# Softplus of the time step on 128 partitions of 68 elements, by way of DRAM, spread over tiles four to ten

## The reference, cut to what matters

```python
xn = rmsnorm(h, lw['norm_mix'])
proj = xn @ lw['w_in']
z, xbc, dt, gate, xl = jnp.split(proj, [s1, s2, s3, s4], axis=-1)
...
dt = jax.nn.softplus(dt + lw['dt_bias'])        # 544 tokens x 16 heads
a = -jnp.exp(lw['a_log'])
y, ssd_h = ssd_chunked(xs, dt, a, bm, cm, ssd_h0)
...
# in ssd_chunked
da = (dt * a).reshape(b, c, q, H).transpose(0, 3, 1, 2)
a_cs = jnp.cumsum(da, axis=-1)                  # in chunks of 128 tokens
decay_states = jnp.exp(a_cs[..., -1:] - a_cs)
...
# in the RG-LRU group
log_a = -LRU_C * r_gate * jax.nn.softplus(-lw['lru_lambda'])   # 1024 channels
```

## Time and profile before

| what | value |
|---|---|
| median of 3 runs | 1906.53 us (1905.66 to 1908.59) |
| the profiled execution | 1902.72 us |
| its span in the profile | 1901.0 us |
| PE busy | 1796.1 us (94%) |
| DVE busy | 1507.3 us (79%) |
| ACT busy | 837.1 us (44%) |
| POOL busy | 522.0 us (27%) |

### The profile page before, as it was taken

One profiled execution on the slowest core, in us unless ns is written; L12 is line 12 of the kernel. 1 busy time (PEld: TensorE's weight loads), 2 busy tenths in 40 slices (PEclk: granted clock), 3 DMA queues, 4 the chain that ended last, 5 costly groups with the idle time before them and its releaser, 6 DMA issues.

```text
span 1901.0 us, 29713 instructions
## 1 busy us (share of the span) xinstructions
PE 1796.1 (94%) x11394; PEld 1732.9 (91%) x11394; DVE 1507.3 (79%) x2723; ACT 837.1 (44%) x1202; POOL 522.0 (27%) x415
## 2 busy tenths in 40 slices
PE   7999969997999999999999999699999999989996
PEld 6999967787999999999999999699999999989995
DVE  7748687566468778999999998678888878888777
ACT  4555562314233333328777777333333333333263
POOL 3100120000000002344544444434444444444300
PEclk9999989999999999999999999899999999999998
DMA  4212332114334446689999999999999999988511
GB/s 143 91 67 79 116 118 99 51 56 179 112 128 146 145 169 227 234 295 345 361 362 373 352 353 359 367 392 376 380 367 380 376 394 379 375 338 340 205 56 48
DMA packets 163772, 462.68 MB, mean 243 GB/s; under 512 B 16624, under 2 KB 76720, under 8 KB 160944
## 3 DMA queue, kind: packets, MB, share of 16 engines
q1 hardware_dynamic: 117552, 292.99, 42.4%
q0 software_dynamic: 46080, 167.79, 23.4%
HBM read 405.46 MB, written 55.27 MB: 242 GB/s over the span
## 4 chain that ended last, share of the span: by engine, by line
PE 71%; DVE 13%; DMA 10%; ACT 3%; issue 2%; SPq 0%; POOL 0%; DVEq 0%; ACTq 0%
PE PS L454 12%; PE PS L1477 8%; PE PS L1478 7%; PE PS L1479 7%; DMA Rw<-vn 7%; PE PS L1490 6%; PE PS L1492 6%; PE PS L1491 6%; PE PS L1466 5%; PE PS L1543 4%; PE PS L2049 2%; DVE Hl L1853 1%; ACT Rh L164 1%; DVE Rl L169 1%; DVE ug L1861 1%
## 5 line engine op out<-in xcount | busy, mean ns | idle before, releaser
L169 DVE TENSOR_TENSOR Rl<-Rw,Rh 128x1024 fp32r<-128x1024 f32 x272 | 332.4, 1223 | 162.2 <-ACT Rh L164 154.8
L164 ACT CAST Rh<-Rw 128x1024 fp32r<-128x1024 f32 x272 | 284.1, 1045 | 389.4 <-PE PS L1492 343.8
L1432 POOL DMA_INDIRECT ug<-un,idxU x160 | 241.6, 1510 | 579.7 <-DVE dots L1861 353.9
L1490 PE MATMUL PS<-Hh,Rh 128*128 128x384 f32 x1024 | 352.2, 344 | 39.3 <-DVE Hl L1853 39.0
L1477 PE MATMUL PS<-Xh,Rh 128*128 128x384 f32 x1016 | 351.2, 346 | 3.8 <-DVE Rl L169 2.8
L1491 PE MATMUL PS<-Hl,Rh 128*128 128x384 f32 x1024 | 349.2, 341 | 0.0
L1492 PE MATMUL PS<-Hh,Rl 128*128 128x384 f32 x1024 | 349.0, 341 | 0.0
L1478 PE MATMUL PS<-Xl,Rh 128*128 128x384 f32 x1016 | 342.3, 337 | 0.0
L1479 PE MATMUL PS<-Xh,Rl 128*128 128x384 f32 x1016 | 341.3, 336 | 0.0
L1432 POOL DMA_INDIRECT ug<-vn,idxU x160 | 234.1, 1463 | 280.6 <-DVE yacc L1866 215.8
L1490 PEld LDWEIGHTS PS<-Hh,Rh 128*128 128x128 f32 x1024 | 194.9, 190 | 48.7 <-issue 48.5
(11 more groups left out here) (426 smaller groups left out, 3126.7 us busy)
## 6 DMA issues: line engine op xcount, KB each, us to landing
Rw<-uw SPq DMA_DIRECT2D x144, 512.0 KB
Rw<-vn SPq DMA_DIRECT2D x128, 512.0 KB
Wr<-wm SPq DMA_DIRECT2D x51, 512.0 KB, 3.3
acts<-Ab SPq DMA_DIRECT2D x128, 192.0 KB
gates<-stg SPq DMA_DIRECT2D x12, 2048.0 KB
Gq<-gates SPq DMA_DIRECT2D x16, 1536.0 KB
Aq<-acts SPq DMA_DIRECT2D x32, 768.0 KB
L<-acsd SPq DMA_DIRECT2D x4, 1024.0 KB, 7.1
```

The lines of the kernel that those rows point to most:

```text
L164: a.copy(self.Rh[:, q, :], self.Rw[:, q, :]).then_inc(self.S("rhi"), 1)
L169: v.tensor_tensor(self.Rl[:, q, :], self.Rw[:, q, :], self.Rh[:, q, :].bitcast(F32), ALU.subtract).then_inc(self.S("rlo"), 1)
L1432: p.indirect_dma_start(out=ug[:, r % 4, :], out_offset=None, in_=un if r < IDC else vn, in_offset=bass.IndirectOffsetOnAxis(ap=idxU[:, r % ...
L1490: pe.matmul(out, Rh[:, q, w], hh, start=(g == 0), stop=False)
```

## The change

The softplus of `dt` runs on 128 partitions x 68 elements instead of 16 x 544 (each head is split over eight partitions). `dtw` becomes [128, 7, 68]. `dts` goes there by way of a DRAM tensor `dtd` (store, wait, load back, after load 3 in SP's list) and comes back by way of `spd` (after load 8). The pieces move: ACT's first from step 2 to 3, DVE's first from 3 to 4, ACT's Ln from 4 to 5, DVE's second from 5 to 6; dt times a, the scan and the differences, which stay on 16 partitions, come at step 8; ACT's exponentials move from step 7 to 9, DVE's last from 8 to 10. A wait before the first sigmoids goes. In the third part of the program, semaphore `cst` is replaced by further counts of `const`.

```diff
-    dtw = at("dtw", A5, [NH, 6, T])
+    dtw = at("dtw", A5, [P, 7, T // 8])
+    dA = at("dA", A5 + T * 4, [NH, T])
...
             load(n)
+            if n == 3:
+                sp.wait_ge(S("dt_v"), 2)
+                sp.dma_start(dtd, dts[:, :]).then_inc(S("dtm"), 16)
+                sp.wait_ge(S("dtm"), 16)
+                sp.dma_start(dtw[:, 6, :], dtd.rearrange("h (q t) -> (h q) t", q=8)).then_inc(S("dtm"), 16)
+            if n == 8:
+                sp.wait_ge(S("spv"), 19)
+                sp.dma_start(spd.rearrange("h (q t) -> (h q) t", q=8), dtw[:, 5, :]).then_inc(S("dtm"), 16)
+                sp.wait_ge(S("dtm"), 48)
+                sp.dma_start(dts[:, :], spd).then_inc(S("dtm"), 16)
...
-            if n == 2:
+            if n == 3:
                 a.preload_act_table(ACT.Exp)
-                a.wait_ge(S("dt_v"), 2)
-                a.activation(dtw[:, 0, :], dts[:, :], ACT.Abs).then_inc(S("spa"), 1)
+                a.wait_ge(S("dtm"), 32)
+                a.activation(dtw[:, 0, :], dtw[:, 6, :], ACT.Abs).then_inc(S("spa"), 1)
...
-            if n == 4:
+            if n == 5:
                 a.wait_ge(S("spv"), 2)
...
-            if n == 7:
+            if n == 9:
                 a.wait_ge(S("spv"), 26)
...
-                if n == GA0 + 1:
-                    a.wait_ge(S("spv"), 27)
...
-            if n == 3:
+            if n == 4:
                 bufs = (lambda q: dtw[:, q, :], lambda q: lv[:, q, :])
...
-            if n == 5:
+            if n == 6:
                 v.wait_ge(w, 12)
...
-                v.scalar_tensor_tensor(out=dts[:, :], in0=dts[:, :], scalar=0.0, in1=dtw[:, 5, :], op0=ALU.max,
-                                       op1=ALU.add).then_inc(w, 1)
+                v.scalar_tensor_tensor(out=dtw[:, 5, :], in0=dtw[:, 6, :], scalar=0.0, in1=dtw[:, 5, :],
+                                       op0=ALU.max, op1=ALU.add).then_inc(w, 1)
...
-                v.tensor_scalar(dtw[:, 4, :], dts[:, :], hv[:, 3:4], None, ALU.mult).then_inc(w, 1)
                 v.tensor_scalar(spl[:, 0, :], lv[:, 5, :], -8.0, None, ALU.mult).then_inc(w, 1)
                 v.tensor_scalar(spl[:, 1, :], lv[:, 5, :], 8.0, None, ALU.mult).then_inc(w, 1)
+            if n == 8:
+                v.wait_ge(S("dtm"), 64)
+                v.tensor_scalar(dA[:, :], dts[:, :], hv[:, 3:4], None, ALU.mult).then_inc(w, 1)
                 v.wait_ge(w, 23)
-                v.tensor_tensor_scan(out=acs[:, :], data0=smask[:, :], data1=dtw[:, 4, :], initial=0.0, op0=ALU.mult,
+                v.wait_ge(S("const"), 28)
+                v.tensor_tensor_scan(out=acs[:, :], data0=smask[:, :], data1=dA[:, :], initial=0.0, op0=ALU.mult,
                                      op1=ALU.add).then_inc(w, 1)
...
-            if n == 8:
+            if n == 10:
                 v.wait_ge(S("spa"), 8)
```

More of the change, by code:

```diff
@@ L253, in mixer @@
     eacd = nc.dram_tensor("eacd", [NC, NH, P], F32, kind="Internal").ap()
+    dtd = nc.dram_tensor("dtd", [NH, T], F32, kind="Internal").ap()
+    spd = nc.dram_tensor("spd", [NH, T], F32, kind="Internal").ap()
     acss = nc.dram_tensor("acss", [NH, 32], F32, kind="Internal").ap()
@@ L1125, in vector @@
                     v.tensor_tensor(b(5), b(5), b(0), ALU.mult).then_inc(w, 1)
-            if n == 5:
+            if n == 6:
                 v.wait_ge(w, 12)
                 v.wait_ge(S("spa"), 7)
-                v.wait_ge(S("const"), 28)
                 for b in bufs:
@@ L1421, in pool @@
         p.iota(iotaX[:, :, :], [[1, TK], [0, 64]], base=0, channel_multiplier=0, allow_small_or_imprecise_dtypes=True
-               ).then_inc(S("cst"), 1)
+               ).then_inc(S("const"), 1)
         p.iota(iota[:, :], [[1, PK]], base=0, channel_multiplier=0, allow_small_or_imprecise_dtypes=True
[L1424 to L1427, removed]
+               ).then_inc(S("const"), 1)
+        p.memset(yacc[:, :], 0.0).then_inc(S("const"), 1)
+        p.memset(yaccS[:, :], 0.0).then_inc(S("const"), 1)
+        p.wait_ge(S("const"), 32)
         for r in range(2 * IDC):
@@ L1867, in row @@
                                        in1=y[:, :], op0=ALU.mult, op1=ALU.add).then_inc(S("sdt"), 1)
-        v.wait_ge(S("cst"), 4)
+        v.wait_ge(S("const"), 32)
         for n in range(NALL):
```

## The result

| kernel | median | lowest to highest | runs |
|---|---|---|---|
| before | 1906.1 us | 1904.52 to 1908.59 | 4 |
| changed | 1891.99 us | 1889.0 to 1900.58 | 4 |

The ratio is 0.9935, its 95% interval 0.9909 to 0.996: 12.4 us faster (8 to 17), where 5.2 was forecast and 1898.8 was the low end of the range. In two later comparisons with more runs the changed kernel stood at 1891.86 and 1892.41 beside a kernel before at 1902.61 and 1903.86, ratio 0.9951 both times (0.9931 to 0.9972, and 0.9933 to 0.9969): 9.3 us.

A forecast was written before the change was run, and what follows sets the result against it. The prediction took PE to bound the first stage, losing up to 6.2 us to late `Wlo` splits, clock and restarts. Less a new 1.0 us stall, 5.2 us off the median 1906.53 gave 1901.3 us, range 1898.8 to 1906.6.

The forecast's parts named there:

- What bounds the kernel, and the 6.2 us that can be won: First stage: PE bounds it; waits for `Wlo`, a slow clock and restarts leave at most 6.2 us to win.
- The blocks on DVE: DVE's softplus blocks: the first falls from 6.7 to 2.0 us, the second from 5.3 to 1.4 us at step 6.
- SP's price, 1.0 us: SP's store of `dts` lands in 2.5 us, delaying load 4; PE stalls 0.7 us before tile 4 plus 0.29 restart.
- Is anything else late: Rest of the first stage: later `Wlo` splits, loads, `dtm` waits and ACT's work all come before PE needs them.
- The shift should go through: After tile 9, ending at 75.8 instead of 81.02 us, later work follows PE, so the end moves too.
- rival 2: Later part, where DMA queues set the pace: the shift is given back; 1906.5 us if whole; chance 0.13.
- the sum, 6.2 - 1.0 = 5.2 us: Whole kernel: first-stage gain less the new stall, against the timed median 1906.53, gives 1901.3 us.
- 1: Rival, before tile 4: a larger new stall and a falling clock leave 2.1 us gain, 1904.4 us; chance 0.14.
- 3: Rival, SP's queue: a landing of up to 10.9 us makes the kernel 4.8 us slower, 1911.3; chance 0.07.
- 4: Rival, DVE: 128 partitions cost more than 16, so its work is not shortened; about 1907.5 us; chance 0.03.
- The chances: Whole kernel: forecast 0.63, the four rivals the rest; as outcomes, faster 0.62, same 0.31, slower 0.07.
- The range: Whole kernel: 1898.8 to 1906.6 us; low end is no stall (1900.3) with half the three runs' spread (1.5 us).

The follow-up runs named there:

- f4: Kernel before, with softplus pieces on 68 of 544 elements and exp in place of the logarithm, no DMA, tensor or step changed: 1895.57 us, ratio 0.9962.
- g3: Changed kernel, but SP stores `dts` three times, waiting for each landing, before going on: 1895.62 us, ratio to before 0.9963.
- e1: Changed kernel without the two DRAM tensors, `dt` going by way of the first slices of `acts`, `gates` at its old place: 1899.31 us, ratio to before 0.998.
- f1: Changed kernel with the two DRAM tensors declared last, so `gates` keeps its old place: 1899.38 us, ratio to before 0.9977.
- f3: Second run of the changed kernel without the two DRAM tensors, `dt` going by way of the first slices of `acts`: 1897.83 us, ratio to before 0.9968.
- f2: Changed kernel unchanged, run again beside the kernel before: 1892.41 us, ratio 0.9951.
- e2: Kernel before, with the two DRAM tensors declared where the change has them and each stored once off the path: 1898.91 us, ratio 0.9984.
- g1: Second run of the kernel before with the change's two DRAM tensors at the same place, each stored once off the path: 1898.21 us, ratio 0.9975.
- g2: Changed kernel with `spd` declared longer, so `gates` begins at 1,048,576: 1900.79 us, ratio to before 0.9992.
- g4: Changed kernel with `spd` declared 96,256 bytes long, so `gates` begins at 290,816: 1892.38 us, ratio to before 0.995.
- e7: Changed kernel with each `vn` load bringing half of its columns, `gates` at the new place: 1879.38 us.
- h1: Changed kernel with the two DRAM tensors declared last (`gates` at its old place) and halved `vn` loads: 1880.52 us.
- e8: Softplus pieces at the changed kernel's steps, but on 16 partitions x 544 without the way over DRAM: 1900.7 us, ratio to before 0.9999.

## Why the prediction was wrong, by its own steps

- *What bounds the kernel, and the 6.2 us that can be won*: right. 6.15 us were won at the first gate matmul; f4 shows the same by another way.
- *The blocks on DVE*: right within 0.1 us each.
- *SP's price, 1.0 us*: mis-sized. It measured 0: the landing was 1.6 us, not the 2.5 that was taken from stores beside a 512 KB load. g3 shows that the mechanism holds.
- *Is anything else late*: right, no new wait for any `Wlo`, and both `dtm` waits were met in time.
- *The shift should go through*: right as far as the last part, which begins at 1225.0 in the mean of the profiles with the short first stage and at 1230.7 with the long one, 5.7 us of 6.2. Of the whole kernel, with `gates` at the old place, e1 gained 3.8 us, f1 4.4, f3 6.1 and f4 7.2, with intervals of 3 to 4 us on either side. So a us or two may be given back (a part of rival 2), and the runs don't show it.
- *The step that failed* is the sum, 6.2 - 1.0 = 5.2 us: it prices the new DRAM tensors as two transfers and puts at nothing, without a reason, that they push `gates` and `acts` along. Placing `gates` 73,728 bytes on brings 5 to 7 us with the changed timing (f1, f3 against f2) and 3 to 5 with the old one (e2, g1). With the 1.0 us of the stall this takes the forecast 5.2 to between 9 and 13, and 9.3 to 12.4 were measured. That the place is the cause is shown; how it works is open. That the four runs of the first comparison gave 12.4 and not 9.3 is within their spread.
- *The rivals*: 1, 3 and 4 did not come, nor was the shift given back whole (2). The chances held no case that was faster than the forecast. The low end at no stall at all left nothing for what the list didn't hold.
- *The range* took the spread of three runs, 3 us, for that of the kernel; 35 runs on one chip (beside e1) show 16.

## What to carry to other kernels

Take the price of a transfer from one that met queues as full or as empty as yours will, and look at the DMA share of its window before using it. A change that declares or resizes a DRAM tensor moves all that are declared behind it: where a part of the kernel is paced by DMA, declare new scratch last, so that nothing else moves (here that was the slower place), or time both orders, before giving the gain to the code. And where PE idles in waits of 2 to 5 us, the runs of one kernel differ by the clock dips that follow; a difference of 0.3% then wants ten runs and more of each (ten to twelve of the changed kernel beside 23 to 35 of the one before still left 3 to 4 us on either side).

## What of the hardware was not expected

- Where two 25 MB tensors (with two small ones) begin in DRAM is worth 7 to 8 us of 1900 (f1 against f2, g2 against g4), all of it in the part whose DMA share is near 1.00. Beside it 1.5 MB loads land in 13.1 to 13.3 against 12.2 us. With halved loads nothing of it is seen (e7 against h1).
- A 34 KB store to DRAM from 16 partitions lands in 1.6 us where the DMA share before it is 0.00, the load back to 128 partitions in runs of 272 bytes in 1.8.
- A gap of 3.18 us (g3) and one of 2.58 (e8) left the clock at full speed, one of 3.64 us was followed by 3.3 us at half, and one of 1.88 us at 1408.90 in the last part by 3.2. So the length of a gap alone does not tell.
